# Block two's RMS scaling inside the stages beside it, and the last tokens' top-k at the end of the first projection

## What is computed

```python
score = jnp.einsum('bqhs,bqh->bqs', jax.nn.relu(jnp.einsum('bqhd,bsd->bqhs', iqb, ik)), iwb)
score = jnp.where(visible[None], score, -jnp.inf)
_, idx = lax.top_k(score, topk)
```

```python
def rmsnorm(x, w):
    xf = x.astype(jnp.float32)
    y = xf * lax.rsqrt(jnp.mean(xf * xf, axis=-1, keepdims=True) + RMS_EPS)
    return (y * w.astype(jnp.float32)).astype(x.dtype)

def modulate(h, shift, scale):
    return h * (1.0 + scale) + shift
```

## Time and profile before

| | us |
| --- | --- |
| median of 3 runs | 3701.42 (3701.0 to 3707.25) |
| profiled execution | 3701.47 |
| its span from first to last instruction | 3699.8 |
| PE busy | 2925.8 (79%) |
| DVE busy | 1625.8 (44%) |
| ACT busy | 990.8 (27%) |
| POOL busy | 781.2 (21%) |
| values stage of layer one of block one | 226.60 to 314.50: 87.90 |
| the same of layer two | 1082.30 to 1170.20: 87.90 |

### The profile page before, as it was taken

The page is one execution under the profiler, slowest core; times in us unless marked ns, Lnnn a source line. Parts: engine busy times, 40 slices in busy tenths (PEclk is TensorE's granted clock), DMA queues, the critical chain, the costliest instruction groups (busy, mean ns, idle before and its releaser), DMA issues. The chain is left out here.

```text
span 3699.8 us, 41514 instructions
## 1 busy us (share of the span) xinstructions
PE 2925.8 (79%) x14576; PEld 2128.8 (58%) x14576; DVE 1625.8 (44%) x3040; ACT 990.8 (27%) x1565; POOL 781.2 (21%) x341
## 2 busy tenths in 40 slices
PE   3986667884995765885697879999897788779997
PEld 3674244232773344332585568888785565657785
DVE  4867632223768643223643652443637214321112
...
PEclk9987886997996876997898999999998888689998
...
DMA packets 98918, 446.00 MB, mean 121 GB/s; under 512 B 16960, under 2 KB 18528, under 8 KB 71648
## 3 DMA queue, kind: packets, MB, share of 16 engines
...
## 5 line engine op out<-in xcount | busy, mean ns | idle before, releaser
L1647 PE MATMUL PS<-one_weights_more,13_h_tokens 128*64 128x512 f32 x832 | 218.6, 634 | 44.1 <-DMA one_weights_more<-in_w_gu 40.2
L221 PE MATMUL PS<-one_mix_h_parts,3_w_part 128*128 128x512 f32 x384 | 161.4, 420 | 84.4 <-DVE one_mix_h_parts L410 84.4
L1647 PEld LDWEIGHTS PS<-one_weights_more,13_h_tokens 128*64 128x64 f32 x832 | 69.8, 145 | 160.5 <-issue 148.7
L1743 DVE SCALAR_TENSOR_TENSOR 13_hid<-13_silu,one_slot_gate,PS 128x256 f32<-128x256 f32 x32 | 15.4, 480 | 332.9 <-ACT 13_silu L1706 332.9
L222 PE MATMUL PS<-one_mix_h_parts,3_w_part 128*128 128x512 f32 x384 | 154.3, 402 | 0.0
L347 POOL TENSOR_TENSOR 9_w_part<-weights_raw,9_w_part 128x1024 fp32r<-128x1024 f32 x16 | 45.4, 2842 | 459.6 <-ACT 9_w_part L320 459.6
L221 PEld LDWEIGHTS PS<-one_mix_h_parts,3_w_part 128*128 128x128 f32 x384 | 74.0, 193 | 106.2 <-ACT 3_w_part L320 85.2
L347 POOL TENSOR_TENSOR 3_w_part<-weights_raw,3_w_part 128x1024 fp32r<-128x1024 f32 x48 | 115.4, 2404 | 78.6 <-ACT 3_w_part L320 78.0
L1601 POOL DMA_INDIRECT one_slot_tokens<-h_rows,one_slot_src x32 | 53.7, 1678 | 342.4 <-PE PS L1633 258.5
L1672 PE MATMUL PS<-one_weights_more,13_hid_turned 128*64 128x512 f32 x432 | 118.4, 598 | 2.2 <-ACT 13_hid_turned L1699 2.2
L226 PE MATMUL PS<-one_mix_h_parts,3_w_part 128*128 128x512 f32 x384 | 98.5, 398 | 12.4 <-POOL 3_w_part L347 12.4
...
## 6 DMA issues: line engine op xcount, KB each, us to landing
...
```

What stands on the lines that cost most here:

```text
L221: nc.tensor.matmul(out, w[0], x[1], start=(j == 0), stop=False)
L1647: mm = nc.tensor.matmul(M.PS[rows(h), 2 + i % 2, :], h_[:, i % 2, k, rows(h)], raw(kind, i, h)[:, k % 4 * 2 * FE:(k % 4 + 1) * 2 * FE], st ...
L1743: nc.vector.scalar_tensor_tensor(out=hid[:, i % 2, :], in0=sl[:], scalar=D_.gate[:, u:u + 1], in1=M.PS[:, 2 + i % 2, FE:2 * FE], op0=ALU.mult,
```

## The change

**Top-k.** `SelectKeys` takes the groups it is to choose and the banks it may use. The last 128 tokens are now chosen in `proj1`: PE does the index products and the first four score products after the ninth rotated pair, with 6 of the 24 chunks behind them; DVE scales the index weights itself, chooses between its 14th and 15th modulation chunk, and then does the last two. In `project_values` the other three groups remain, each group's scores issued one chunk earlier than before.

**RMS.** The five `rms_modulate` blocks and the block that stored the output are gone. Before block 17's projection a short block `rms_stats` computes only the reciprocal roots `M.rs`. The other four are computed in the `gemm_residual` before (`Stats`): ACT squares each updated piece, POOL adds the first 7 squares up one after the other, PE sums over features twice (the gathered squares and the last) by products of 32 columns, ACT and DVE take root and reciprocal on 128 columns in place of 512 or 768, PE spreads them and ACT copies them out. The normalising, scaling, shifting and splitting (`Norm`) now stand in the opening of the projection or `gated_up`: DVE multiplies, ACT shifts and rounds, DVE makes the low part. To let PE begin as pieces arrive, the first two chunks are multiplied together, piece by piece (`first_pair`), when both chunks have their high and low part. The final norm multiplies and stores in four parts. Block numbers fall by one from the second feed-forward part on (23 becomes 22, 28 becomes 27, 39 becomes 36).

The diff, cut to its core:

```diff
-    def highs(self, act, out, early=None):
+    def highs(self, act, out, early=None, both=False):
         self.high(act, 0, 0, 1)
+        if both:
+            self.high(act, 1, 1, 1)
         if early:
             early()
         whole = self.pairs if self.N % 2 else self.pairs - 1
-        if whole > 0:
-            with act.Fori(0, whole) as i:
+        if both:
+            out(0, 0)
+            self.high(act, 2, 0, 2)
+            out(1, 1)
+        if whole > both:
+            with act.Fori(int(both), whole) as i:
...
+    def first_pair(self, pe, terms, spans, done):
+        pe.wait_ge(self.s["high_done"], 2)
+        pe.wait_ge(self.s["split_done"], 2)
+        for a in range(spans):
+            for k in range(KD):
+                pe.wait_ge(self.s[done], a * KD + k + 1)
+                for u in range(2):
+                    for out, w, x in terms(u, a, k):
+                        self.nc.tensor.matmul(out, w[0], x[1], start=(k == 0), stop=False)
+                        self.nc.tensor.matmul(out, w[0], x[0], start=False, stop=False)
+                        mm = self.nc.tensor.matmul(out, w[1], x[0], start=False, stop=(k == KD - 1))
+                    if a == spans - 1 and k == KD - 1:
+                        mm.then_inc(self.s["used"], 1)
...
+        if between:
+            if end < between[0]:
+                loop(end, between[0], None)
+            between[1](pe)
+            end = between[0]
...
-            S.multiply(pe, chunk, rotate, 1, PAIRS)
-            pe.wait_ge(s["wi"], 16)
-            for t in range(TT):
-                for k in range(KD):
-                    mm = nc.tensor.matmul(M.PS[:, 6, t * NH_I:(t + 1) * NH_I], h[:, k, t * P:(t + 1) * P],
-                                          WI[:, k, :], start=(k == 0), stop=(k == KD - 1))
-            mm.then_inc(s["index_done"], 1)
+            def index(pe):
+                pe.wait_ge(s["wi"], 16)
+                for t in range(TT):
+                    for k in range(KD):
+                        mm = nc.tensor.matmul(M.PS[:, 6, t * NH_I:(t + 1) * NH_I], h[:, k, t * P:(t + 1) * P],
+                                              WI[:, k, :], start=(k == 0), stop=(k == KD - 1))
+                mm.then_inc(s["index_done"], 1)
+                pe.wait_ge(s["turned"], 2 + N_ROPE)
+                keys.scores(pe, 0)
+            S.multiply(pe, chunk, rotate, 1, PAIRS, (PAIRS + 1, index))
...
-            act.wait_ge(s["index_done"], 1)
-            nc.scalar.activation(B.iw[:], M.PS[:, 6, 0:TT * NH_I], ACT.Copy, scale=NH_I ** -0.5 * HD ** -0.5)
         @block.vector
         def _(dve):
                     turn(2 * i + u, u)
                     R.chunks(dve, i - 1, u)
             turn(N_ROPE - 1, 0)
-            for n in range(N_ROPE // 2 * 2 - 2, MODS):
+            MIDDLE = MODS - 2
+            for n in range(N_ROPE // 2 * 2 - 2, MIDDLE):
+                R.chunks(dve, n // 2, n % 2)
+            dve.wait_ge(s["rot_done"], N_ROPE + 1)
+            dve.wait_ge(s["index_done"], 1)
+            nc.vector.tensor_scalar(B.iw[:], M.PS[:, 6, 0:TT * NH_I], NH_I ** -0.5 * HD ** -0.5, None,
+                                    ALU.mult).then_inc(s["iw_done"], 1)
+            dve.wait_ge(s["iw_done"], 1)
+            keys.choose(dve)
+            for n in range(MIDDLE, MODS):
                 R.chunks(dve, n // 2, n % 2)
             R.plus_one(dve, MODS, (2, 4, 5))
-            dve.wait_ge(s["rot_done"], N_ROPE + 1)
...
+    def square(self, act, k, each=False):
+        if k >= 3:
+            act.wait_ge(self.s["stat"], k - 2 if each else max(1, k - 3))
+        self.nc.scalar.activation(self.sq[:, k % 3, :], self.M.xT[:, k, 0:self.TW],
+                                  ACT.Square).then_inc(self.s["squared"], 1)
+    def gather(self, pool, k):
+        pool.wait_ge(self.s["squared"], k + 1)
+        if k > 1:
+            pool.wait_ge(self.s["stat"], k - 1)
+        self.nc.gpsimd.tensor_tensor(self.acc, self.acc if k > 1 else self.sq[:, 0, :], self.sq[:, k % 3, :],
+                                     ALU.add).then_inc(self.s["stat"], 1)
+    def add(self, pe, src, first, last):
+        for b in range(self.TW // P):
+            j, c = 32 * (b % 4), b // 4
+            mm = self.nc.tensor.matmul(self.M.PS[j:j + 32, c, 0:P], self.M.K[:, K_MEAN:K_MEAN + 32],
+                                       src[:, b * P:(b + 1) * P], start=first, stop=last)
+        mm.then_inc(self.s["stat"], 1)
+    def add_each(self, pe):
+        for k in range(KD):
+            pe.wait_ge(self.s["squared"], k + 1)
+            self.add(pe, self.sq[:, k % 3], k == 0, k == KD - 1)
+    def add_gathered(self, pe):
+        pe.wait_ge(self.s["stat"], KD - 2)
+        self.add(pe, self.acc, True, False)
+        pe.wait_ge(self.s["squared"], KD)
+        self.add(pe, self.sq[:, (KD - 1) % 3], False, True)
...
+    def roots(self, act):
+        act.wait_ge(self.s["stat"], KD)
+        for c, rows in self.groups():
+            self.nc.scalar.activation(self.sd[0:rows, c, :], self.M.PS[0:rows, c, 0:P], ACT.Sqrt,
+                                      bias=self.M.eps[0:rows, 1:2]).then_inc(self.s["sd"], 1)
+        act.wait_ge(self.s["spread"], 1)
+        for c, rows in self.groups():
+            n = rows // 32
+            self.nc.scalar.activation(self.M.rs[:, c * 4 * P:c * 4 * P + n * P].rearrange("p (b q) -> p b q", q=P),
+                                      self.M.PS[:, 4:4 + n, c * P:(c + 1) * P], ACT.Copy)
+    def inverses(self, dve):
+        for c, rows in self.groups():
+            dve.wait_ge(self.s["sd"], c + 1)
+            self.nc.vector.reciprocal(self.sd[0:rows, c, :], self.sd[0:rows, c, :]).then_inc(self.s["rstd"], 1)
...
+        def low(n):
+            out, shift, t = self.part(n, 1)
+            dve.wait_ge(s["h_high"], n + 1)
+            nc.vector.scalar_tensor_tensor(out=out, in0=t, scalar=shift, in1=self.part(n, 0)[0].bitcast(F32),
+                                           op0=ALU.add, op1=ALU.subtract).then_inc(s["h_done"], 1)
...
+        for n, (a, k) in enumerate(self.order):
+            t0, nt, _ = self.spans[a]
+            nc.vector.scalar_tensor_tensor(out=self.t[:, n % 4, 0:nt], in0=M.xT[:, k, t0:t0 + nt],
+                                           scalar=self.ws[:, a, k:k + 1], in1=M.rs[:, t0:t0 + nt],
+                                           op0=ALU.mult, op1=ALU.mult).then_inc(s["norm"], 1)
+            if n:
+                low(n - 1)
+        low(len(self.order) - 1)
+    def shifts(self, act):
+        for n in range(len(self.order)):
+            out, shift, t = self.part(n, 0)
+            act.wait_ge(self.s["norm"], n + 1)
+            self.nc.scalar.activation(out, t, ACT.Identity, bias=shift).then_inc(self.s["h_high"], 1)
...
+            for n in range(KD):
+                S.low(pool, n, n % 2)
+                if ride and n >= 2:
+                    R.load_next(pool, n // 2, n % 2)
+                if n >= 4:
+                    sums.gather(pool, n - 3)
+            for k in (KD - 3, KD - 2):
+                sums.gather(pool, k)
         @block.scalar
         def _(act):
             if mix is not None:
                 for k in range(KD):
                     nc.scalar.activation(src[:, 0, k], mix[:, k, :], ACT.Copy).then_inc(s["h_high"], 1)
-            S.highs(act, lambda n, u: None, (lambda: R.sigmoid(act)) if ride else None)
+            if not stats:
+                S.highs(act, lambda n, u: None, (lambda: R.sigmoid(act)) if ride else None)
+                return
+            def square(k):
+                act.wait_ge(s["scaled"], NS * (k + 2))
+                sums.square(act, k)
+            for n in range(KD):
+                S.high(act, n, n % 2, n // 2 + 1)
+                if ride and n == 0:
+                    R.sigmoid(act)
+                if n >= 2:
+                    square(n - 2)
+            square(KD - 2)
+            square(KD - 1)
+            sums.roots(act)
...
+            for k in range(0, KD, 2):
+                sp.wait_ge(s["norm"], k + 2)
+                sp.dma_start(out[:, k:k + 2], M.xT[:, k:k + 2, 0:T]).then_inc(s["stored"], 16)
+            sp.wait_ge(s["stored"], 16 * (KD // 2))
...
-                    K.scores(pe, n)
+                    if n + 1 < TT:
+                        K.scores(pe, n + 1)
...
-            with ExitStack() as first:
-                M.hT = tensor(first, "ab_hT", [P, KD, TA])
-                rms_modulate(nc, M, A["norm_mix"][0], both, 0, 1)
+            rms_stats(nc, M, TA)
             ride = (modulation(A, DEPTH, 4), A["b_ada"][DEPTH], A["cond"][1], 2 * KD, 4, KD)
-            project(nc, M, proj_weights(A, DEPTH), 12, B.PT, [(0, T), (T, TC)], ab_v, ride=ride, parts=(4,))
+            project(nc, M, proj_weights(A, DEPTH), 12, B.PT, [(0, T), (T, TC)], ab_v, ride=ride, parts=(4,),
+                    norm=(A["norm_mix"][0], both, 0, 1, B.V[:, 0:2].rearrange("p t (u v) -> p (t u) v", v=T)))
...
...
```

252 lines of the change are left out of this document (146 added, 106 removed).

## The result

| | before | after |
| --- | --- | --- |
| median | 3701.21 (3695.01 to 3707.25, 4 runs) | 3591.05 (3575.53 to 3603.58, 4 runs) |
| ratio | | 0.970, 95% interval 0.966 to 0.974 |
| profiled execution, its span | 3699.8 | 3590.2 |
| PE busy | 2925.8 (79%) | 2872.6 (80%) |
| DVE busy | 1625.8 (44%) | 1677.8 (47%) |

The change gives back 110 us. The four executions of the changed kernel differ by 28 us among themselves, so the terms are read from the two profiles and not from whole times.

The account below looks back on a forecast made before the run. DVE's choosing bounds the values stages and a serial chain block two's boundaries; elsewhere PE or the weights bound. Savings of 44.6 + 11.8 + 2.0 + 4.8 + 8.0 + 11.5 = 82.7 us give 3619, range 3597 to 3653.

Parts of the forecast that it names:

- Top-k: Values stages 63 us instead of 87.9, first projections 2.6 longer: 44.6 us saved over two layers, between 29 and 57.
- Block 16: Stats block before block 17's projection: 22.7 us instead of 34.6, with sums at 8 x 1.9, so 11.9 won.
- rival 2: Sums' 32-column products run side by side in the array: 0.5 us a piece instead of 1.9, giving 3602; chance 0.12.
- The tails: Norm work after each gemm_residual's last update of x: 9.3 us, 6.8 at 512 tokens, and 1 for a boundary.
- 28 to 31: Block two, old numbering: POOL's additions slow block 28 by 5 us, 19.8 won; net gain 4.8, between -8 and 15.
- The openings: Normalising moved into the next block delays its products: 12.3 us lost in old block 23, 9.9 in 17, 12.9 in 39.
- Rival 1: The openings' three normalising steps run in series, 2.3 us a piece instead of 1.45, giving 3643; chance 0.22.
- Rivals 3 and 4: 3: lower PE clock makes the kernel slower, 3742, chance 0.04; 4: choice still paces the values stage, 3657, chance 0.05.

Follow-up runs that it names:

- sums_wide: Changed kernel with block 16's sums made 128 columns wide, each in its own bank: 13.04 us for 96 passes, stats block 18.7 us instead of 12.3.
- thin_gather: Changed kernel with POOL's additions of squares cut to 32 columns: 84.0 us from the start of block 27 to that of 29, against 90.2.

## Why the prediction was off

**The places were right.** The values stage was bounded by DVE's choosing, the boundaries of block two by a chain with no products in it, and outside these only stages whose length follows PE's clock moved by more than 1.3 us (the attention stages by 2.7, and block 30, 1.5 longer with the clock at 0.94 for 1.00).

**Top-k: right in mechanism, 8 too high** (36 without the attention's share, for 44.6; the 41.6 of the table is nearer by luck). PE got to the third group's scores at 36.9 us where the forecast had 36.6, held by the bank. But from there to the end it needed 29.6 us where the sum had 26.4: the four score products themselves, taken bank by bank (267.66 to 270.73), find no room in its 24.9 for two chunks. So the stage took 66.5 instead of 63. And the first projections lost 4 and 6 instead of 2.6 each: DVE's end there was put too early, as its last operation of the choice shares SBUF with POOL (2.2 us at 220.46 for 0.69) as well. The forecast put DVE's loss to POOL in the values stage at 6.6; it was 8.0 in the two additions and 1.8 in the comparison at 264.37, which stands right before the bank is freed.

**Block 16: the step that failed most, by 10.4 us.** It priced a sum at 0.157 us a pass, in series, from attention products that wait between themselves, so that its busy time holds the full length of passes that nothing follows. `sums_wide` shows the honest price of such a product done back to back: 0.11 at full clock and 0.21 at the lower one, 13.0 us in all where the sum had 15.2. And rival 2 was true: in column groups a set of 12 passes costs four rounds, 0.44 us, where the rival had 0.5. So of the 10.4 us, 6.4 are the column groups (18.7 against 12.3, where ACT's squares pace it) and 4.0 are the row chosen and handovers put too high. I had written down the mechanism, but at 0.12 beside a main case that a row seemed to carry; the row was of another situation.

**The tails: 1.9 to 2.6 us each too dear, mostly for the same reason.** 7.7 instead of 10.3 with its boundary in 21, 5.4 instead of 7.8 in 35, and 17.2 for 19.1 at the end. In 21 the sums are 0.71 for 1.9 and the spreading 1.23 for 1.9.

**28 to 31: 9.5 us.** The 5 us for POOL's additions are right (6.2 by `thin_gather`); missing was that the block before already lost 5.5 us in the same slot to a weight subtraction, which ACT's new order moves away. A cost was added and the one that goes was not taken off: the block's last update ends 1.0 us later and not 5. The rest is the tail and an opening of 12.3 for 15.

**The openings: right within 3 us.** 13.9, 8.0, 12.3, 11.5 lost for 12.3, 9.9, 15, 12.9. PE starts at 12.5 for 13.2 in 22. Rival 1 (the chain in series) is out: a piece of 512 takes 1.33 us on DVE in block 29.

**The range** held only the errors of the top-k term and of the rivals one by one. Block 16 and all four tails shared one price per pass, so that its error came in five times: 10.4, and 1.9 to 2.6 at each tail. Rival 2 (3602 by the forecast's own figures) with the upper bound of the top-k term would already have been 3590, under the low end that was stated. With rival 2 taken through and the missed collision of block 28, some 5 us, the forecast would have been 3597 for the 3591 measured. Of that rest 5.4 us are the attention stages, where the change has no part, and what agrees beyond it does so by errors that cancel: top-k 8 too high, and block 16's handovers, the spreading and three of the openings too dear.

Rivals 3 and 4 did not occur: PE's granted clock was 0.95 and more from 5 us after its start in block 22's opening, and the values stage did not stay near 82.
